# First sliding-attention scores inside the z projection, and two weight chunks split by ScalarE and VectorE instead of GpSimd

## The reference

```python
u = rmsnorm(h, norm_mix)
proj = u @ w_in
aq, ak, av, dq, dk, dv, dz, db, da = jnp.split(proj, split_idx, axis=-1)
aq, ak = rope(aq, positions), rope(ak, positions)
attn_out = sliding_window_sink_attention(aq, ak, av, sinks)   # 8 heads of 64, 2 key heads, window 128
dn_out = gated_deltanet(dq, dk, dv, dz, db, da, ...)          # uses silu(z) only at its end
h = h + jnp.concatenate([attn_out, dn_out], axis=-1) @ w_o
```

```python
s = einsum('bnhgqk', q, [previous block, own block]) * 64 ** -0.5
s = where(valid, s, -inf)
probs = softmax(concatenate([s, sink], -1))[..., :-1]
o = einsum('bnqhgd', probs, v)
```

## Time and profile before

| | us |
|---|---|
| median of 3 runs | 2065.48 |
| lowest and highest | 2061.72, 2065.75 |
| the profiled execution | 2057.51 |
| its span | 2055.7 |
| busy: PE, DVE, ACT, POOL | 1955.4, 1352.1, 921.0, 525.8 |
| mean granted clock of TensorE | 0.971 |

### The profile page before, as it was taken

How to read it: one execution, slowest core, us unless ns; L and a number is a source line. 1 busy time by engine, 2 the same in 40 slices (tenths; PEclk the granted TensorE clock), 3 DMA queues, 4 the chain that set the end, 5 groups by cost and what they waited for, 6 DMA issues and landing times. The chain is left out here.

```text
span 2055.7 us, 24085 instructions
## 1 busy us (share of the span) xinstructions
PE 1955.4 (95%) x8922; PEld 1586.1 (77%) x8922; DVE 1352.1 (66%) x1421; ACT 921.0 (45%) x1002; POOL 525.8 (26%) x270
## 2 busy tenths in 40 slices
PE   7998999999999999999999999998999999999993
PEld 6876887888888878768887686887887888888882
DVE  5438756667674659344044572747989999999994
ACT  2233424423323451241002213235878888878873
POOL 3522013000000004616653553610112222223222
PEclk9998999999999999999999999989999999999996
DMA  5311011665554222242335271331999999999994
GB/s 171 109 62 62 29 27 41 208 201 190 189 195 134 92 94 79 77 180 85 100 102 225 64 262 43 126 134 65 349 362 373 373 368 374 378 379 378 369 358 154
DMA packets 115163, 388.51 MB, mean 189 GB/s; under 512 B 21333, under 2 KB 23668, under 8 KB 88334
## 3 DMA queue, kind: packets, MB, share of 16 engines
q1 hardware_dynamic: 98656, 353.00, 47.6%
q10 hardware_dynamic: 10382, 25.42, 3.9%
q0 software_dynamic: 6048, 9.03, 1.2%
HBM read 355.06 MB, written 45.35 MB: 195 GB/s over the span
## 5 line engine op out<-in xcount | busy, mean ns | idle before, releaser
L2847 DVE TENSOR_TENSOR m_lo<-m_raw,m_hi 128x2048 fp32r<-128x2048 f32 x200 | 449.0, 2285 | 8.1 <-ACT m_hi L2775 7.9
L2775 ACT ACTIVATE m_hi<-m_raw 128x2048 fp32r<-128x2048 f32 x200 | 383.3, 1923 | 102.7 <-DMA m_raw<-in_w_exp_gate_dram 65.3
L264 PE MATMUL ps<-xhi,whi 128*128 128x512 f32 x936 | 374.6, 400 | 8.8 <-DVE xlo L457 5.8
L266 PE MATMUL ps<-xhi,wlo 128*128 128x512 f32 x936 | 366.4, 391 | 0.0
L265 PE MATMUL ps<-xlo,whi 128*128 128x512 f32 x936 | 366.3, 391 | 0.0
L241 POOL TENSOR_SCALAR whi<-raw 128x2048 fp32r<-128x2048 f32 (+1 forms) x57 | 108.4, 1902 | 897.1 <-PE ps L266 757.6
L243 POOL TENSOR_TENSOR wlo<-raw,whi 128x2048 fp32r<-128x2048 f32 (+1 forms) x57 | 263.8, 4627 | 4.8
L264 PE MATMUL ps<-m_hi,xt_hi 128*128 128x512 f32 x544 | 218.7, 402 | 4.8 <-DVE xt_lo L2852 3.6
L264 PEld LDWEIGHTS ps<-xhi,whi 128*128 128x128 f32 x936 | 177.0, 189 | 52.2 <-issue 10.1
L265 PE MATMUL ps<-m_lo,xt_hi 128*128 128x512 f32 x544 | 215.6, 396 | 0.0
L266 PE MATMUL ps<-m_hi,xt_lo 128*128 128x512 f32 x544 | 214.1, 394 | 0.0
(11 more groups left out here) (470 smaller groups left out, 3134.0 us busy)
## 6 DMA issues: line engine op xcount, KB each, us to landing
m_raw<-in_w_exp_gate_dram SPq DMA_DIRECT2D x68, 1024.0 KB, 5.4
m_raw<-in_w_exp_up_dram SPq DMA_DIRECT2D x68, 1024.0 KB, 5.3
m_raw<-in_w_exp_down_dram SPq DMA_DIRECT2D x68, 1024.0 KB, 5.0
raw<-in_w_in_dram SPq DMA_DIRECT2D x42, 1024.0 KB, 5.2
ada_w<-in_w_ada_dram ACTq DMA_DIRECT2D x48, 512.0 KB, 4.2
y_rows<-xhi SPq DMA_DIRECT2D x39, 512.0 KB, 7.0
raw<-in_w_up_dram SPq DMA_DIRECT2D x16, 1024.0 KB, 5.7
raw<-in_w_down_dram SPq DMA_DIRECT2D x16, 1024.0 KB, 5.1
```

The source lines that it names most:

```text
L264: nc.tensor.matmul(o, lh, rh, start=start, stop=False)
L266: return nc.tensor.matmul(o, ll, rh, start=False, stop=stop)
L2775: nc.scalar.activation(m_hi[s][:], m_raw[s][:], ACT.Copy).then_inc(m_split, 1)
L2847: nc.vector.tensor_tensor(m_lo[s][:], m_raw[s][:], m_hi[s][:].bitcast(F32), ALU.subtract).then_inc(m_low, 1)
```

## The change

1. **PE.** `scores(0)` moves from behind the z projection into its first half, behind tile 3 (a third entry of `inside`). It writes banks 4 and 5 in place of 0 and 1 (`score_bank`), waits for the key pad and the ropes, and no longer for the Silu. `scores(1)` waits for all four Silus, as before.
2. **DVE.** `shifted(0)` stands directly behind the last rope. Then comes `chunk_low` of chunk 12, then `normed(1)` to `normed(7)` and the gate instructions, then `shifted(1)`, `chunk_low` of chunk 13, and `normalised(0)`.
3. **ACT.** `chunk_high` of chunk 12 stands behind that of chunk 11; then `exps(0)`, the four Silus, `chunk_high` of chunk 13, and unit 0's copies. One more table load comes with it.
4. **POOL** no longer splits chunks 12 and 13.

```diff
+        def score_bank(i):
+            return 2 * (i % 2) if i else 4
...
-                done_split[0] = Z_CHUNK + 1
-                pool.wait_ge(split_done, Z_CHUNK + 1)
-                stream_split(pool, PHASE["win"])
+                done_split[0] = Z_CHUNK + 3
+                pool.wait_ge(split_done, Z_CHUNK + 3)
+                stream_split(pool, PHASE["win"] - 2)
...
-                linear(pe, U_dz, (xhi, xlo), inside=[((0, 1), lambda: swap_key(0)), ((0, 2), lambda: swap_key(1))])
...
                 def scores(i):
                     n, g = AU[i]
                     if i >= 2:
                         pe.wait_ge(*soft.at("mask", i - 2))
-                    else:
-                        pe.wait_ge(lin_free[side(U_dz)], 4 * nth(U_dz) + 2 * i + 2)
+                    elif i == 1:
+                        pe.wait_ge(lin_free[side(U_dz)], 4 * nth(U_dz) + 4)
...
+                def first_scores():
+                    pe.wait_ge(key_pad, 1)
+                    pe.wait_ge(rope_done, TT + AKV)
+                    scores(0)
+                linear(pe, U_dz, (xhi, xlo), inside=[((0, 1), lambda: swap_key(0)), ((0, 2), lambda: swap_key(1)), ((0, 3), first_scores)])
...
-                pe.wait_ge(key_pad, 1)
-                pe.wait_ge(rope_done, TT + AKV)
-                scores(0)
...
                 chunk_high(act, Z_CHUNK)
-                for m in range(4):
-                    act.wait_ge(lin_full, 4 * U_dz + m + 1)
-                    nc.scalar.activation(delta_in[:, 12 + m, :], bank(U_dz, m), ACT.Silu).then_inc(lin_free[side(U_dz)], 1)
-
+                act.wait_ge(split_done, Z_CHUNK + 1)
+                chunk_high(act, Z_CHUNK + 1)
...
+                exps(0)
+                for m in range(4):
+                    act.wait_ge(lin_full, 4 * U_dz + m + 1)
+                    nc.scalar.activation(delta_in[:, 12 + m, :], bank(U_dz, m), ACT.Silu).then_inc(lin_free[side(U_dz)], 1)
+                act.wait_ge(split_done, Z_CHUNK + 2)
+                chunk_high(act, Z_CHUNK + 2)
...
-                exps(0)
...
                 rope_key(1)
-                for r in range(1, 8):
-                    normed(r)
...
+                shifted(0)
+                chunk_low(dve, Z_CHUNK + 1)
+                for r in range(1, 8):
+                    normed(r)
...
-                for i in range(len(AU)):
+                for i in range(1, len(AU)):
                     shifted(i)
+                    if i == 1:
+                        chunk_low(dve, Z_CHUNK + 2)
```

More of the change, by code:

```diff
@@ L952, in scores @@
                         r = slice(AHD * (h % 2), AHD * (h % 2) + AHD)
-                        last = nc.tensor.matmul(ps[:, 2 * (i % 2) + h % 2, 2 * P * (j // 2):2 * P * (j // 2) + 2 * P],
+                        last = nc.tensor.matmul(ps[:, score_bank(i) + h % 2, 2 * P * (j // 2):2 * P * (j // 2) + 2 * P],
                                                 qT[r, h // 2, n * P:n * P + P], kT[r, g, n * P:n * P + 2 * P],
@@ L1530, in _ @@
                 rope_key(1)
-                for r in range(1, 8):
-                    normed(r)
-                dve.wait_ge(gate_act, 4)
-                own(4, nc.vector.tensor_tensor(pos, pos, gate_t[:, 4], ALU.add))
-                own(5, nc.vector.scalar_tensor_tensor(step[:], pos.rearrange("p (t h) -> p t h", h=GH), -1.0,
-                                                      a_log[:].unsqueeze(1).to_broadcast([P, TT, GH]), ALU.mult, ALU.mult))
-                own(6, nc.vector.tensor_scalar(gate_t[:, 5], gate_t[:, 5], 1.0, None, ALU.add))
-                own(7, nc.vector.reciprocal(beta[:], gate_t[:, 5].rearrange("p (t h) -> p t h", h=GH)))
                 dve.wait_ge(sink_in, 16)
@@ L1552, in shifted @@
                     for par in range(2):
-                        src = ps[:, 2 * (i % 2) + par, :].rearrange("p (a n) -> p a n", n=2 * P)
+                        src = ps[:, score_bank(i) + par, :].rearrange("p (a n) -> p a n", n=2 * P)
                         dst = s.rearrange("p (a b) n -> p b a n", b=2)[:, par]
@@ L1565, in shifted @@
                     nc.vector.tensor_tensor(gap, sinks[:, 4 * g:4 * g + 4], row_max, ALU.subtract).then_inc(soft.sem, 1)
+                shifted(0)
+                chunk_low(dve, Z_CHUNK + 1)
+                for r in range(1, 8):
+                    normed(r)
+                dve.wait_ge(gate_act, 4)
+                own(4, nc.vector.tensor_tensor(pos, pos, gate_t[:, 4], ALU.add))
+                own(5, nc.vector.scalar_tensor_tensor(step[:], pos.rearrange("p (t h) -> p t h", h=GH), -1.0,
+                                                      a_log[:].unsqueeze(1).to_broadcast([P, TT, GH]), ALU.mult, ALU.mult))
+                own(6, nc.vector.tensor_scalar(gate_t[:, 5], gate_t[:, 5], 1.0, None, ALU.add))
+                own(7, nc.vector.reciprocal(beta[:], gate_t[:, 5].rearrange("p (t h) -> p t h", h=GH)))
                 def normalised(i):
```

## The result

| | before | after |
|---|---|---|
| the comparison: median of 5 runs each, us | 2061.72 | 2049.68 |
| lowest and highest | 2058.54, 2065.75 | 2042.91, 2057.10 |
| ratio, 95% interval | | 0.9937 [0.9914, 0.9961] |
| profiled execution, its span | 2057.51, 2055.7 | 2049.68, 2047.8 |

What follows compares the result with a forecast made beforehand. It took PE's 7.14 us hole, from DVE stalled by POOL, and its clock fall as the cost, with DVE bounding the later attention. 6.9 us up to `shifted(2)` plus 0.6 made 7.5; 2065.48 became 2058.0, range 2053 to 2063.5.

Steps and rivals of the forecast that it cites:

- the hole: PE's 7.14 us wait for unit 0's exponentials behind the first scores; claimed to vanish, with the clock fall inside it.
- The steps up to `shifted(2)`: Scores inside z, unit 0 on DVE and ACT, work behind unit 1: `shifted(2)` starts at 179.3 instead of 186.25, 6.9 us less.
- D: Time from the start of the last rope (L558 writing kT) to `shifted(2)`'s mask; forecast 22.6 us.
- the step: From `shifted(2)` to `shifted(3)` on DVE; claimed to go from 5.65 to 5.06 us, 0.6 less.
- DVE's low half of chunk 13: Behind `shifted(1)`; the one part of POOL's removed work claimed to come back on the path, 2.3 us.
- The ropes: At the scores inserted in z; PE should not wait for them, margin 0.3 us, any lateness adding one for one.
- the middle: From `shifted(3)` to the last unit's transposes; the prediction claimed no change for these units.
- the end: From the last unit's transposes to the first beta matmuls on PE; the prediction had no term for it.
- DVE bounds the rest of the attention, and the change adds nothing to those units: Attention from 190 to 218: DVE busy 25.92 of 28 us, PE 23.33, so no gain or loss forecast there.
- The clock falls all the same: Rival: PE's remaining holes of about 1 us drop the clock at 174, leaving 3.4 us gain, 2062.1; chance 0.20.
- The slow clock throughout: Rival: clock falls at 174 and stays low through the attention's seven units left, 14.9 us slower, 2080.4; chance 0.05.
- The gain reached the end: Opposite of a rival: something timed otherwise, such as a weight, takes the wait over, 2065.5; chance 0.06.

Runs made afterwards that it cites:

- late_low: Changed kernel with chunk 13 split at the end of the attention, high half on ACT, low half on DVE; 2053.7 us, ratio 0.9938 to the kernel before.
- the 29: All timed runs of the changed kernel, the later batches included; median 2051.37 us.
- the first batch: First four follow-up kernels, timed beside the kernel before, which has 35 runs there with median 2063.03 us.
- scores_only: Changed kernel with chunks 12 and 13 split on POOL again, as before the change; 2056.96 us, ratio 0.9972 to the kernel before.
- scores_warm: scores_only with 9 unused matmuls in PE's hole of 2.46 us ahead of unit 1's transposes; 2050.81 us, ratio 0.9949 to the kernel before.
- warm_tail: Kernel before with 7 unused matmuls in the last unit's two PE holes; 2059.73 us, ratio 0.9996 to the kernel before.
- after_third: Changed kernel, unedited, for a third follow-up trace; 2051.26 us, ratio 0.9951 to the kernel before.
- after_fifth: Changed kernel, unedited, a single execution for a fifth trace; 2059.78 us.

## Why the prediction was right or wrong

**What held.** The reading of the hole held: DVE stalled by POOL's low halves, the norms in front of unit 0, the clock falling in the hole. The steps up to `shifted(2)` held too, within 0.4 us. Counted from the last rope I had unit 0's mask at 2.3 (159.0 less 156.76), it was 2.33; z's last Silu 1.5 us later, it was 1.29; D at 22.6, it is 22.19; the step at 5.06, it is 5.06. DVE's low half of chunk 13 cost 2.2 us on the path (2.3 in the sum), which late_low shows by taking it off. The ropes were in time.

The sum had 6.9 for D and 0.6 for the step, 7.5 in all. The means of the traces have 7.3, 1.9, -0.7 in the middle and 2.3 at the end, 10.8 in all.

**What failed, first: "the step of 5.65 becomes 5.06: 0.6".** The term was mis-sized. It took the fall in the hole from one execution. D is fixed, since the fall lies inside the hole, where PE idles; but when the clock comes back varies, and the step was 5.65, 8.27, 5.76 and 8.27 in four traces, a mean of 6.99. The term is 1.9, not 0.6. The windows showed it: 0.84 in 158 to 200 in the trace that I had, 0.72 in the next.

**Second: "DVE bounds the rest of the attention, and the change adds nothing to those units".** This left out the last unit, and for unit 2 it was wrong: the low half of chunk 13 makes a hole of 1.76 us ahead of unit 2's transposes, and behind it the clock fell in two of six executions. The row of the last unit was there: the window 218 to 220 at 0.76, and I used it as evidence for a rival without asking what it cost before, or whether it would be there after. It costs 9.17 - 5.99 = 3.2 to 4.3 us where it comes. In the means the last unit is worth 2.3 us to the change, and against that stand 0.7 us in the middle, mostly the two falls in unit 2. That the means favour the change at the last unit may be luck, as said above.

**Third: the base.** With three runs from 2061.72 to 2065.75 the median stood 3.0 us over the one of 103 runs. The profiled execution lay 8 us under it, and I took this for a reason to stretch the range down to 2053, when it meant that the median itself was a few us uncertain. Over the 35 runs of the first batch the kernel before spreads from 2050.72 to 2073.49. Base and gain erred to the same side, 3.0 + 3.6, and the range had room for one of them. The remaining 1.7 us, by which the five runs lie under the 29, are scatter.

**The rivals.** "The clock falls all the same" came true in three of six traces of the changed kernel, twice in unit 2 and once at the last unit, never at 174 where I had put it, at 2.7 to 4.1 us each (I had 4.1). Nearest to that place it came in scores_only, at 178.4, behind 2.46 us of idle, and cost 3.4 to 3.7 us (8.80 less the 5.36 of scores_warm, or less 5.06). It didn't bring the time back to "same", since the kernel before has such falls too, and more of them: a rival about a state that both kernels can be in must be priced in both. The page "TensorE: Matmul & The Clock Gate" of the Trainium skill (section "Why this matters for your kernels") puts such drops on long idle gaps between bursts of matmuls. The traces agree for 7.14 and 4.42 us. They don't for 1.22 and 1.76, behind which the clock fell in some executions and stayed in others; the measurement decides. The slow clock throughout did not come. The gain reached the end, though 2.7 to 3.3 us of it were lost behind the stretch in three of six executions, in which the clock fell again near 323.

## What to carry to other kernels

A hole on PE costs twice, once by its length and once by the clock behind it, and the second part differs from execution to execution: take it from several traces, of both kernels if you can, before it goes into a sum. Ask of a moved piece of work not only whether it leaves the path but what hole it leaves on PE: here scores_warm and the change gain the same as far as the runs can tell, one by filling the hole and one by shortening it. And where three runs spread over 4 us, a difference of 7 has to be forecast with a range that lets the base move too.

## What the runs showed of the hardware

- The clock fell at the last unit behind a hole of 1.22 us in some executions of the same program and not in others, with D equal to 0.01 us in all. After 7.14 us of idle it had fallen in all five traces (four of the kernel before, and warm_tail), after 4.42 and after 2.46 us in the one trace with such a hole.
- Not only POOL's low half stalls DVE. In scores_only DVE's L1568, 128x16, takes 1.76 us from 170.10 to 171.86, beside POOL's high half, 169.94 to 171.84. In the changed kernel it takes 0.17. ACT's high half beside DVE stalls nothing: in the trace before, a last step of a rope (L558, 128x512, both inputs in SBUF) takes 0.69 us from 146.15, beside the high half from 145.40 to 147.31, and 0.69 us from 142.29 without it.
- Much of the scatter goes with the granted clock. Of the 98 runs of the kernel before that were timed in the batches, the 49 with a mean granted clock of 0.969 or less have a median of 2065.39 us, the 17 with 0.973 or more one of 2055.66.
- Executions with the same stretch still differ behind it. after_third and after_fifth have sums of 61.48 and 61.41 and times of 2053.35 and 2059.78. At the `y_out` memset of DVE (L2891) after_third is still the later one, at 1420.58 against 1419.31, so the difference arises behind it, in the mixture of experts. What makes it there isn't shown.
